# The memory tokens' preparation in the gate projection, and two memory key steps among attention's last steps

## What is computed

```python
y_diff = diff_attention(q, k, v, cos, sin, lam, subln_w[l], lambda_init)
mixed = jnp.concatenate([y_ssd, y_diff], axis=-1) @ w_out[l]
x = x + rms_norm(mixed, norm_mix_post[l])
h = rms_norm(x, norm_mem_q[l])
mem_h = rms_norm(mem, norm_mem_kv[l])
c = cross_attention(h, mem_h, w_mq[l], w_mk[l], w_mv[l], w_mo[l])
```

## Time and profile before

| | us |
|---|---|
| median of 3 runs | 1451.37 |
| the runs | 1449.99 to 1452.27 |
| time of the profiled execution | 1451.05 |
| span of its instructions | 1449.3 |
| PE busy | 1419.9 (98%) |
| DVE busy | 951.7 (66%) |
| ACT busy | 662.7 (46%) |

### The profile page before, as it was taken

The page is one execution under the profiler, slowest core; times in us unless marked ns, Lnnn a source line. Parts: engine busy times, 40 slices in busy tenths (PEclk is TensorE's granted clock), DMA queues, the critical chain, the costliest instruction groups (busy, mean ns, idle before and its releaser), DMA issues.

```text
span 1449.3 us, 19683 instructions
## 1 busy us (share of the span) xinstructions
PE 1419.9 (98%) x7280; PEld 1188.1 (82%) x7280; DVE 951.7 (66%) x1559; ACT 662.7 (46%) x1298; POOL 92.5 (6%) x132
## 2 busy tenths in 40 slices
PE   9999999999989999999999989999999999999998
PEld 7889888886669988888888878888888888888886
DVE  4883565628877634543654798887776685467898
ACT  6324222327776523533533665444555464454443
POOL 1000000000001101010000360000000000000011
PEclk9999999999999999999999999999999999999999
DMA  9212111102003612311231433664343797766463
GB/s 322 60 32 59 30 30 30 44 15 88 1 1 117 221 71 87 116 59 42 75 116 45 140 115 117 222 203 178 146 152 131 255 360 251 259 220 198 150 233 129
DMA packets 94607, 185.52 MB, mean 128 GB/s; under 512 B 10161, under 2 KB 28593, under 8 KB 92465
## 3 DMA queue, kind: packets, MB, share of 16 engines
q1 hardware_dynamic: 87312, 153.30, 31.4%
q10 hardware_dynamic: 7200, 30.97, 6.4%
HBM read 142.30 MB, written 41.94 MB: 127 GB/s over the span
## 4 chain that ended last, share of the span: by engine, by line
PE 88%; DVE 4%; ACT 3%; issue 3%; DMA 1%; SPq 1%; POOL 0%; ACTq 0%; DVEq 0%; POOLq 0%
PE ps L2185 26%; PE ps L2187 26%; PE ps L2186 26%; PE ps L2386 1%; PE ps L2244 1%; PE ps L2425 1%; PE ps L2327 1%; DMA x_in<-in_x_dram 1%; PE ps L2405 1%; ACT probs L1013 1%; DVE wq_l L1930 1%; DVE nmax L1662 1%; PE ps L2345 1%; PE ps L2330 1%; ACT junk L853 0%
## 5 line engine op out<-in xcount | busy, mean ns | idle before, releaser
L2185 PE MATMUL ps<-wh,oph 128*128 128x512 f32 (+1 forms) x576 | 214.9, 373 | 0.0
L2187 PE MATMUL ps<-wh,opl 128*128 128x512 f32 (+1 forms) x576 | 211.0, 366 | 0.0
L2186 PE MATMUL ps<-wl,oph 128*128 128x512 f32 (+1 forms) x576 | 210.3, 365 | 0.0
L2185 PE MATMUL ps<-d_ring 128*128 128x512 f32 x448 | 174.3, 389 | 0.0
L2187 PE MATMUL ps<-d_ring 128*128 128x512 f32 x448 | 174.3, 389 | 0.0
L2186 PE MATMUL ps<-d_ring 128*128 128x512 f32 x448 | 174.3, 389 | 0.0
L780 POOL TENSOR_TENSOR rms<-stat,mhalf 128x1 f32<-128x1 f32 (+2 forms) x59 | 56.2, 954 | 1307.1 <-DVE stat L1393 1285.4
L2187 PEld LDWEIGHTS ps<-wh,opl 128*128 128x128 f32 x576 | 108.1, 188 | 17.9
L2185 PEld LDWEIGHTS ps<-wh,oph 128*128 128x128 f32 x576 | 108.2, 188 | 16.7 <-ACT vt L973 0.2
L2186 PEld LDWEIGHTS ps<-wl,oph 128*128 128x128 f32 x576 | 108.4, 188 | 16.5
L1311 ACT ACTIVATE d_ring<-left_raw 128x512 fp32r<-128x512 f32 x112 | 70.2, 627 | 94.9 <-PE ps L2187 75.5
(11 more groups left out here) (362 smaller groups left out, 2923.2 us busy)
## 6 DMA issues: line engine op xcount, KB each, us to landing
right_raw<-in_w_down_dram SPq DMA_DIRECT2D x128, 256.0 KB, 4.0
u_kept_s<-us SPq DMA_DIRECT2D x64, 256.0 KB, 3.0
left_raw<-u_kept_s SPq DMA_DIRECT2D x64, 256.0 KB, 2.9
w_blk<-in_w_up_blocks_dram ACTq DMA_DIRECT2D x14, 1024.0 KB, 5.8
left_raw<-u_kept_a SPq DMA_DIRECT2D x48, 256.0 KB, 3.1
raw<-in_w_in_dram SPq DMA_DIRECT2D x16, 512.0 KB, 3.8
u_kept_a<-u SPq DMA_DIRECT2D x24, 256.0 KB, 2.2
x_in<-in_x_dram SPq DMA_DIRECT2D x8, 512.0 KB, 9.4
```

What stands on the lines that cost most here:

```text
L2185: te.matmul(o, lh, rh, start=first, stop=False)
L2186: te.matmul(o, lh, rl, start=False, stop=False)
L2187: return te.matmul(o, ll, rh, start=False, stop=last)
```

## The change

- The load of the memory tokens and of their gain moves from the start of attention into the gate projection (n = 52); the squares move to n = 54 and 55, the means to n = 56, the norm to n = 57 and 58, PE's transposes to the ends of n = 59 and 60, ACT's high parts to n = 60 and 61, DVE's low parts to n = 61 and 62. The norm works in place in `h_mem`, now in region TMP. The squares' unused output goes to PSUM, and the transposes to banks 4, 5, 6 and 3.
- PE waits for the memory tokens' low parts before the first scores, no longer after attention.
- The memory key steps 0 and 1 stand on PE in attention's iterations NS and NS + 1, in the places where the transposes of the memory tokens were issued at the end of an iteration, but now at its beginning.
- PE's loop after attention starts at n = 2. Block T(m) is transposed after step 2m + 2, no longer after step 2m + 1; T7 stays after step 15. ACT's and DVE's loops over the 16 steps are not changed.

```diff
--- before.py
+++ after.py
@@ -174,6 +174,7 @@
 Y_DONE = 57
+MEM_LOAD, MEM_SQUARE, MEM_NORM, MEM_TR = 52, 54, 57, 59
@@ -186,9 +187,11 @@
-def tr_bank(n):
-    return 2 * (n - TR_MEM) if TR_MEM <= n < TR_MIX else 4 + 2 * (n % 2)
+def tr_bank(n, b):
+    if TR_MEM <= n < TR_MIX:
+        return ((4, 5), (6, 3))[n - TR_MEM][b]
+    return 4 + 2 * (n % 2) + b
@@ -303,9 +306,7 @@
-        m_in = at("m_in", "OPL", 0, [P, 2, D])
-        h_mem = at("h_mem", "OPL", 8192, [P, 2, D])
-        m_junk = at("m_junk", "OPL", 16384, [P, D])
+        h_mem = at("h_mem", "TMP", 8192, [P, 2, D])
@@ -991,17 +992,28 @@
+                if n == MEM_LOAD:
+                    act.wait_ge(ssd_b, NT)
+                    act.wait_ge(ssd_y, NT)
+                    act.wait_ge(ssd_h, NT)
+                    for i in range(MT):
+                        act.dma_start(h_mem[:, i, :], t["mem"][0][i * P:(i + 1) * P, :]).then_inc(x_loaded[i], 16)
+                    act.dma_start(gain_b[:], rows(t["norm_mem_kv"][0:1, :])).then_inc(gain_b_loaded, 16)
+                if 0 <= n - MEM_SQUARE < MT:
+                    i = n - MEM_SQUARE
+                    act.wait_ge(x_loaded[i], 16 * 3)
+                    square(("mem", i), h_mem[:, i, :], ps[:, 6:8, :].rearrange("p b c -> p (b c)"))
                 if n >= Y_DONE:
                     i = n - Y_DONE
                     act.wait_ge(gate_done, i + 1)
-                    square(("y", i), mix[:, 0:4, i * P:(i + 1) * P], junk[:, 0:512].rearrange("p (k c) -> p k c", k=4))
+                    square(("y", i), mix[:, 0:4, i * P:(i + 1) * P], ps[:, 7, :].rearrange("p (k c) -> p k c", k=4))
+                if 0 <= n - MEM_TR - 1 < MT:
+                    i = n - MEM_TR - 1
+                    tr_hi(TR_MEM + i, memh[:, :, i * P:(i + 1) * P])
@@ -1043,10 +1051,6 @@
-                if n == NS + 1:
-                    mem_hi(0)
-                if n == NS + 2:
-                    mem_hi(1)
@@ -1061,9 +1065,6 @@
-                if n in (6, 7):
-                    act.wait_ge(x_loaded[n - 6], 16 * 3)
-                    square(("mem", n - 6), m_in[:, n - 6, :], m_junk[:])
@@ -1643,6 +1644,17 @@
+                if n == MEM_SQUARE + MT:
+                    for i in range(MT):
+                        squares(("mem", i))
+                        mean(("mem", i), D)
+                if 0 <= n - MEM_NORM < MT:
+                    i = n - MEM_NORM
+                    dve.wait_ge(gain_b_loaded, 16)
+                    normalise(("mem", i), TR_MEM + i, h_mem[:, i, :], gain_b[:], h_mem[:, i, :])
+                if 0 <= n - MEM_TR - 2 < MT:
+                    i = n - MEM_TR - 2
+                    tr_lo(TR_MEM + i, memh[:, :, i * P:(i + 1) * P], meml[:, :, i * P:(i + 1) * P])
@@ -1702,17 +1714,6 @@
-                if n == NS + 2:
-                    for i in range(MT):
-                        tr_lo(TR_MEM + i, memh[:, :, i * P:(i + 1) * P], meml[:, :, i * P:(i + 1) * P])
-                if n == 8:
-                    for i in range(MT):
-                        squares(("mem", i))
-                        mean(("mem", i), D)
-                if n == 9:
-                    dve.wait_ge(gain_b_loaded, 16)
-                    for i in range(MT):
-                        normalise(("mem", i), TR_MEM + i, m_in[:, i, :], gain_b[:], h_mem[:, i, :])
@@ -2361,6 +2362,13 @@
+                if 0 <= n - MEM_TR < MT:
+                    i = n - MEM_TR
+                    pe.wait_ge(ssd_y, NT)
+                    pe.wait_ge(ssd_h, NT)
+                    pe.wait_ge(ssd_bcb, NT)
+                    pe.wait_ge(rt_ev, 2 * NT)
+                    transpose_tile(TR_MEM + i, lambda k: h_mem[:, i, k * P:(k + 1) * P])
@@ -2372,6 +2380,7 @@
             pe.wait_ge(ssd_bcb, NT)
+            pe.wait_ge(lo_done, 2 * (TR_MEM + MT))
@@ -2412,11 +2416,17 @@
                 if n < NS:
                     scores(n)
+                if n in (NS, NS + 1):
+                    for c in range(2):
+                        pe.wait_ge(ex_done[c], NS - 1)
+                    feature_step("mk", n - NS, memh, meml, n - NS, 0, MEM)
                 if 2 <= n < NS + 2:
                     probs_transpose(n - 2, 0)
                 if n >= 3:
                     k = n - 3
                     i, h = steps[k]
+                    if k == 0:
+                        pe.wait_ge(sq_done, SQ[("y", NT - 1)] + 1)
@@ -2427,22 +2437,19 @@
-                if n in (NS, NS + 1):
-                    mem_tile(n - NS)
-            pe.wait_ge(lo_done, 2 * (TR_MEM + MT))
-            for n in range(16):
+            for n in range(2, 16):
                 name, st = STEPS[STEP0["mk"] + n]
                 if name == "mk":
                     feature_step("mk", st, memh, meml, st % 2, 0, MEM)
                 else:
                     feature_step("mv", st, memh, meml, st % 2, 0, MEM)
-                if n % 2:
-                    i = MIX_TILES[n // 2]
-                    transpose_tile(TR_MIX + n // 2, lambda k: mix[:, k, i * P:(i + 1) * P])
+                for m in ([n // 2 - 1] if n % 2 == 0 else [7] if n == 15 else []):
+                    i = MIX_TILES[m]
+                    transpose_tile(TR_MIX + m, lambda k: mix[:, k, i * P:(i + 1) * P])
```

More of the change, by code:

```diff
@@ L216 @@
 O_NORM_AT = {2 * m - 1: m for m in range(2, NT)}
-POWS = ([("in", 0)] + [("y", i) for i in range(NT)] + [("mem", i) for i in range(MT)]
+POWS = ([("in", 0)] + [("mem", i) for i in range(MT)] + [("y", i) for i in range(NT)]
         + [("o", i) for i in MIX_TILES])
@@ L858, in tr_hi @@
                     act.wait_ge(tr_done, 2 * n + b + 1)
-                    s.activation(dst[:, 4 * b:4 * b + 4], ps[:, tr_bank(n) + b, :].rearrange("p (k c) -> p k c", k=4),
+                    s.activation(dst[:, 4 * b:4 * b + 4], ps[:, tr_bank(n, b), :].rearrange("p (k c) -> p k c", k=4),
                                  ACT.Copy).then_inc(hi_done, 1)
@@ L996, in _ @@
                     act.wait_ge(gate_done, i + 1)
-                    square(("y", i), mix[:, 0:4, i * P:(i + 1) * P], junk[:, 0:512].rearrange("p (k c) -> p k c", k=4))
+                    square(("y", i), mix[:, 0:4, i * P:(i + 1) * P], ps[:, 7, :].rearrange("p (k c) -> p k c", k=4))
+                if 0 <= n - MEM_TR - 1 < MT:
+                    i = n - MEM_TR - 1
+                    tr_hi(TR_MEM + i, memh[:, :, i * P:(i + 1) * P])
             steps = ATT_STEPS
             NS = len(steps)
-            def mem_hi(i):
-                tr_hi(TR_MEM + i, memh[:, :, i * P:(i + 1) * P])
             def attn_exp(n, c):
@@ L1016, in _ @@
             act.wait_ge(pj_done, STEP0["z"] + 16)
-            for i in range(MT):
-                act.dma_start(m_in[:, i, :], t["mem"][0][i * P:(i + 1) * P, :]).then_inc(x_loaded[i], 16)
-            act.wait_ge(ssd_b, NT)
-            act.dma_start(gain_b[:], rows(t["norm_mem_kv"][0:1, :])).then_inc(gain_b_loaded, 16)
             act.dma_start(gain_a[:], rows(t["norm_mix_post"][0:1, :])).then_inc(gain_a_loaded, 16)
@@ L1402, in tr_lo @@
                     v.tensor_tensor(dst_l[:, 4 * b:4 * b + 4],
-                                    ps[:, tr_bank(n) + b, :].rearrange("p (k c) -> p k c", k=4),
+                                    ps[:, tr_bank(n, b), :].rearrange("p (k c) -> p k c", k=4),
                                     dst_h[:, 4 * b:4 * b + 4].bitcast(F32), ALU.subtract).then_inc(lo_done, 1)
@@ L2243, in transpose_tile @@
                     for k in range(4):
-                        ins = te.transpose(ps[:, tr_bank(n) + b, k * P:(k + 1) * P], src(4 * b + k), ident[:])
+                        ins = te.transpose(ps[:, tr_bank(n, b), k * P:(k + 1) * P], src(4 * b + k), ident[:])
                     ins.then_inc(tr_done, 1)
@@ L2390, in scores @@
                     te.matmul(ps[:, score_bank(i, c) + i // 4, kn - P:kn], ident_b[:], mask_q[:], start=False, stop=True).then_inc(s_done[c], 1)
-            def mem_tile(i):
-                pe.wait_ge(ex_done[0], NS)
-                pe.wait_ge(ex_done[1], NS)
-                transpose_tile(TR_MEM + i, lambda k: h_mem[:, i, k * P:(k + 1) * P])
             def probs_transpose(k, part):
```

## The result

| | before | after |
|---|---|---|
| median, us | 1451.29 | 1486.01 |
| the runs, us | 1449.83 to 1452.27 (6) | 1484.14 to 1489.19 (6) |
| span of the profiled execution | 1449.3 | 1484.3 |

The ratio is 1.0245, with an interval from 1.023 to 1.026: slower by 34.7 us, where 23.1 were predicted, and 1.0 above the range's upper end. The mean granted clock of the six executions after the change goes with their times: 0.987 and 0.988 in the two shortest (1484.14 and 1484.77), 0.984 in the two longest (1489.08 and 1489.19). So the clock takes more from some executions of this kernel than from others, and the profile shows one of them (1486.13, 0.986).

What follows compares the result with a forecast made beforehand. PE, busy in 98% of the span, was taken to bound the kernel. Terms 1.6 + 1.2 - 2.5 + 3.7 + 1.6 + 18.8 - 1.3 gave 23.1 us on 1451.37: forecast 1474.5 us, range 1470 to 1485.

Steps and rivals of the forecast that it cites:

- gate projection and start of attention, to the first exponential: Gate projection takes 16 memory-token transposes, +1.6; first scores then wait for the tokens' low parts, +1.2.
- attention, to the end of step 28's product: Inside attention, two squares leave ACT and two norms leave DVE, shortening two long pairs of steps: -2.5 us.
- end of attention until T0, with the clock: After attention, step 2 waits for weights split behind gain_q's load, +3.7; half clock behind that wait, +1.6.
- loop, T0 to T6: Memory steps' loop: six periods grow from 6.63 to 9.8 us, 58.8 against 39.94, so +18.8.
- until `wo`: From T6 to the first output projection step, only step 15 and T7 remain: -1.3 us.
- behind it: After the start of the output projection, everything is bound by PE and moves as a whole: no change.
- the loop's mechanism: In the loop, step 2m + 4 waits for weights whose split is queued on ACT behind T(m)'s copies; PE idles 3.0.
- the forecast's own marks, s + 3.7 and s + 6.86: In the loop, counted from block start s: step 2m + 3 ends at s + 3.7, step 2m + 4 starts at s + 6.86.
- PE's clock after that wait: Behind the 5.5 us idle ahead of step 2, PE runs at half clock for 3.2 us: +1.6.
- the first rival: PE's clock falls in each of the loop's six waits of 3.0: 6 x 1.6 = 9.6, giving 1484.1; chance 0.15.
- the start of attention: First scores wait for the memory tokens' last low parts on DVE, ready at about 333.7: +1.2, bounds 0 and 2.6.

Runs made afterwards that it cites:

- The two experiments that part transposes and splits: Changed kernel with block transposes where they stood before: 1453.86 us; changed kernel with only ACT's and DVE's copies of the blocks two iterations later: 1455.14 us.
- the run with 12 matmuls: Changed kernel plus 12 useless identity matmuls on PE in each of the loop's six waits: 1474.95 us, ratio 1.0157.
- 8 matmuls of filler: Changed kernel plus 8 useless identity matmuls on PE in each of the loop's six waits: 1475.85 us, one execution.
- the last two kernels: Changed kernel with block copies later, gain_q's load and second key unit's splits earlier; with memory tokens' copies moved to n = 60: 1447.80 us, without: 1450.42 us.
- 4 of filler: Changed kernel plus 4 useless identity matmuls on PE in each of the loop's six waits: 1479.04 us, one execution.
- the start's copies moved: Changed kernel with ACT's and DVE's copies of the memory tokens moved to the end of gate projection iteration n = 60: 1484.88 us, ratio 1.0233.
- the first experiment: Changed kernel with PE's block transposes where the kernel before had them, T0 ahead of memory step 2: 1453.86 us, ratio 1.0015.

## Why the prediction was wrong, point by point

The sum stood at 23.1 us; the span grew by 35.0. Measured at the same marks, in us against the profile of before:

| term | predicted | measured | from |
|---|---|---|---|
| gate projection and start of attention, to the first exponential | +2.8 | +4.6 | 334.34, 338.94 |
| attention, to the end of step 28's product | -2.5 | -2.8 | 433.86, 435.70 |
| end of attention until T0, with the clock | +5.3 | +5.0 | 447.67, 454.55 |
| loop, T0 to T6 | +18.8 | +29.6 | 39.94, 69.56 |
| until `wo` | -1.3 | -0.9 | 7.41, 6.48 |
| behind it | 0 | -0.6 | spans |

**Right: the loop's mechanism and its size at full clock.** The six waits for `wl` came at the foreseen place, and 2.95 each for the foreseen 3.0. (By the forecast's own marks, s + 3.7 and s + 6.86, it would be near 3.2; the period doesn't depend on it.) The two experiments that part transposes and splits, each from its own side, take them away. With the clock held at 1.00 the loop takes 58.83 for 58.8.

**Wrong: the clock behind the waits of 3.0.** The step that failed is the one under *PE's clock after that wait* and the first rival. It priced a fall once, for the wait of 5.5, and left the six of 3.0 at a chance of 0.15, because each is shorter than the 3.17 of the earlier trace rows. In the trace the clock fell behind five of them. The price was too low as well: 1.6, half of the one slow stretch in the earlier trace rows, where the five cost 10.7, that is 2.15 each (69.56 less the 58.83 of the run with 12 matmuls, over five), since the half clock can last through the whole of step 2m + 4 (5.26 for 2.94). That is 10.7 of the 11.9 by which the span's growth of 35.0 exceeds the sum. The rival's number, 1484.1, came near with the wrong parts: six falls at 1.6 are 9.6, five at 2.15 are 10.7.

**Wrong: the start of attention.** PE's start was foreseen at 333.7 and came at 333.80. But the clock fell behind this wait of 2.23 too, which no term held, and the eight scores took 1.69 longer. With attention's overshoot and the smaller terms the account closes: 1.8 - 0.3 - 0.3 + 10.8 + 0.4 - 0.6 = 11.8.

**Right: attention and its end.** The two long pairs, 8.18 and 8.21 before, are 7.14 and 6.63 (starts 364.23, 371.37, 378.00). Step 2 stood 14.54 us behind step 28's product, by the forecast 14.64. The table `gain_q` and the two splits were last there, as it said.

**Wrong, and too small to matter: what follows moves as a whole.** Behind the start of `wo` the kernel is 0.6 shorter. Before, the wait of 2.05 at 836.50 kept the clock and the one of 3.17 at 868.98 lost it. The first row is of the kernel before, the other two are the same two waits after the change:

```profile
836.50 0.50 PE L2185 MATMUL ps<-oph,wq_h 128*128 128x512 f32 x1 [2.05 <-DVE wq_l L1930]
...
872.40 0.50 PE L2186 MATMUL ps<-oph,wq_h 128*128 128x512 f32 x1 [2.05 <-DVE wq_l L1931]
...
905.05 0.47 PE L2186 MATMUL ps<-oph,wq_h 128*128 128x512 f32 x1 [1.72 <-DVE u_s L1985]
```

Now the clock falls at the first of the two waits. PE then takes longer, but the second wait ends when DVE is done, so it shrinks from 3.17 to 1.72, and the distance between the two hardly changes (32.48 before, 32.65 after). Behind the shorter wait the clock stays at 1.00. So a fall ahead of a wait for another engine can cost next to nothing.

**What bound the range.** The forecast took the one wait at either side of its case (1.59 kept, 3.17 lost) as a rule of length, and gave the clock in every wait a chance of 0.15 though 3.0 is nearer to the one that lost it. Two rows can't carry that: the wait of 2.05 went both ways at one place.

The Trainium skill (TensorE: Matmul & The Clock Gate, section HAM oscillation) describes a loop in which each round's wait makes the next burst start throttled. This case's trace agrees for five rounds of six at 2.95 us of wait, for two of six at 2.06, for none of six at 1.17. The section's example has waits of about 3 to 5 us; that shorter ones do it too, at times, is this case's finding.

## What to carry to other kernels

Where a change makes an engine wait in each round of a loop, follow the split or copy it waits for through the queue of the engine that makes it; whichever of the two is moved away from the other, the wait goes. Price a long wait of PE as its length plus a clock that may fall behind it: here it fell behind 24 of 26 waits of 2.95 and more and behind 15 of 32 from 1.84 to 2.48, and a fall in the loop cost 1.5 to 2.3. Put such falls into the forecast itself rather than into a rival. Then ask whether a later wait for another engine takes the loss in. A filler of useless matmuls, shorter than the wait, tells in one run what of a loss is wait and what is clock.

## What the hardware showed

How often PE's clock stayed at 1.00 or was at 0.50 behind a wait, counted over the profiles of all 13 kernels, from the start of attention on:

| wait, us | kept | fell | where |
|---|---|---|---|
| 1.16 to 1.33 | 14 | 0 | 8 matmuls of filler (6); first weights of `wo` (7); before, at 373.77 |
| 1.43 | 2 | 1 | end of attention, in three kernels |
| 1.59 | 1 | 0 | before, end of attention |
| 1.69 to 1.73 | 6 | 0 | the place of 905.05 after, in five kernels; T0 with the transposes as before |
| 1.84 | 1 | 1 | the last two kernels, step 2 |
| 2.05 to 2.07 | 11 | 8 | 4 of filler (6); the place of 836.50 before, in 13 kernels |
| 2.23 | 5 | 4 | start of attention, in nine kernels |
| 2.35, 2.48 | 0 | 2 | transposes as before: at 873.23 and step 2 |
| 2.95 | 2 | 10 | the loop, after and with the start's copies moved |
| 3.12 to 3.17 | 0 | 7 | the place of 868.98 before, in seven kernels |
| 5.3 to 5.4 | 0 | 7 | step 2, in seven kernels |

Each of the 40 falls in these profiles stands at such a wait. From 1.84 on the share of falls rises with the length, but equal waits at equal places went both ways. What else decides stays open; none of the runs varied it alone.

The cost of a fall differed as much. At the start of attention the eight scores took 0.9 to 1.7 us longer (2.84 in the first experiment, 3.68 after the change, for 1.99). In the loop a period took 1.5 (4 of filler) to 2.3 longer. At the end of attention, behind the wait of 1.43, it was 3.7, and ahead of the wait at 905.05 next to nothing.

A matmul of 128 columns in plain float32 is recorded as two rows here (x40 for twenty), a transpose as one. Twenty identity matmuls kept PE for 4.63 us; twenty transposes of the same identity, which this kernel uses as a filler of its own at the start of attention, took 2.35:

```profile
333.78 2.35 PE L2412 MATMUL ps<-ident 128*128 128x128 f32 x20
```

That row is of the kernel before. A filler must be sized by its own row.
